# Taking two unread products out of the router stages of a hybrid decoder step

## The reference

```
u      = rmsnorm(h, norm_ffn[l]) * (1 + scale2) + shift2
g      = top-1 of 4 groups by softmax(u @ rg_w + rg_b)
e      = top-2 of the 4 experts of that group by softmax(u @ re_w + re_b)
weight = g_val * e_val / sum(e_val)
h1, h3 = u @ w1[expert], u @ w3[expert]          # 1024 -> 512
h      = h + gate2 * sum(weight * (silu(h1) * h3) @ w2[expert])
```

## Time and profile before

| what | value |
|---|---|
| device time, median of 3 runs | 963.4 us (963.22 to 965.36) |
| span of the profiled execution, first to last instruction | 961.9 us |
| TensorE busy in it | 908.2 us, 94% |
| TensorE weight loads | 498.1 us, 52% |
| VectorE busy | 321.1 us, 33% |
| ScalarE busy | 173.7 us, 18% |
| transfers | 316.22 MB, mean 329 GB/s |
| the product of `idle`, layer 0 | from 331.7 us, 4 instructions |
| the product of `idle`, layer 1 | from 711.6 us, 4 instructions |

### The profile page before, as it was taken

One profiled execution on the slowest core, in us unless ns is written; L12 is line 12 of the kernel. 1 busy time (PEld: TensorE's weight loads), 2 busy tenths in 40 slices (PEclk: granted clock), 3 DMA queues, 4 the chain that ended last, 5 costly groups with the idle time before them and its releaser, 6 DMA issues.

```text
span 961.9 us, 13150 instructions
## 1 busy us (share of the span) xinstructions
PE 908.2 (94%) x5368; PEld 498.1 (52%) x5368; DVE 321.1 (33%) x801; ACT 173.7 (18%) x385; POOL 40.0 (4%) x68
## 2 busy tenths in 40 slices
PE   6999999998889899999999989999989999999985
PEld 3665665453556654444444357776764444444533
DVE  3241135446524531112111077468462111211016
ACT  3200000022322221111111040173131110011103
POOL 0000000003300000000000110000000000000020
PEclk9999999998999999999999999999999999999998
DMA  9967987887977569999999987233848999999991
GB/s 374 420 282 263 352 311 265 323 312 264 402 288 306 219 241 421 424 420 421 422 421 423 377 333 279 88 134 135 350 176 335 417 422 421 423 423 420 422 358 66
DMA packets 47623, 316.22 MB, mean 329 GB/s; under 512 B 5602, under 2 KB 6002, under 8 KB 12354
## 3 DMA queue, kind: packets, MB, share of 16 engines
q1 hardware_dynamic: 39456, 288.90, 73.9%
q0 software_dynamic: 6096, 22.30, 6.4%
q10 hardware_dynamic: 2002, 4.08, 1.2%
HBM read 303.84 MB, written 11.42 MB: 328 GB/s over the span
## 4 chain that ended last, share of the span: by engine, by line
PE 78%; DMA 7%; SPq 6%; DVE 5%; issue 2%; ACT 1%; POOL 0%; POOLq 0%; DVEq 0%
PE banks L822 26%; PE banks L1446 14%; PE banks L1491 8%; PE banks L1405 7%; SPq L421 6%; PE banks L899 5%; DMA ring<-in_ew 3%; DMA scr<-in_ew 3%; PE banks L831 2%; PE banks L886 2%; PE banks L1462 1%; PE banks L907 1%; PE banks L939 1%; PE banks L963 1%; PE banks L1506 1%
## 5 line engine op out<-in xcount | busy, mean ns | idle before, releaser
L822 PE MATMUL banks<-uT,ring 128*128 128x320 f32 x448 | 124.5, 438 | 2.6 <-DVE uT L1700 2.6
L1446 PE MATMUL banks<-ring,scr 128*64 128x512 f32 x512 | 113.0, 593 | 1.7 <-issue 1.7
L822 PEld LDWEIGHTS banks<-uT,ring 128*128 128x128 f32 x448 | 85.6, 192 | 42.4 <-issue 7.0
L1405 PEld LDWEIGHTS banks<-scr 128*128 128x128 f32 (+1 forms) x768 | 75.3, 190 | 14.5 <-issue 12.4
L1446 PE MATMUL banks<-scr 128*64 128x512 f32 x352 | 78.1, 593 | 3.7 <-DMA scr<-in_ew 3.7
L1405 PE MATMUL banks<-scr 128*128 128x128 f32 (+1 forms) x768 | 81.4, 281 | 0.0
L1446 PEld LDWEIGHTS banks<-ring,scr 128*64 128x64 f32 x512 | 37.5, 137 | 74.6 <-issue 73.7
L619 ACT ACTIVATE scr<-banks,mods 128x128 f32<-128x128 f32 x128 | 36.5, 367 | 171.9 <-PE banks L1405 171.9
L1927 DVE TENSOR_TENSOR scr<-scr,banks 128x512 f32<-128x512 f32 x16 | 11.0, 687 | 156.7 <-ACT scr L605 156.7
L1491 PE MATMUL banks<-scr,uT 128*64 128x512 f32 x256 | 57.1, 596 | 0.0
L822 PE MATMUL banks<-ring,uT 128*128 128x512 f32 x128 | 57.1, 599 | 0.0
(11 more groups left out here) (381 smaller groups left out, 922.4 us busy)
## 6 DMA issues: line engine op xcount, KB each, us to landing
ring<-in_ew SPq DMA_DIRECT2D x112, 1024.0 KB, 21.2
ring<-in_w SPq DMA_DIRECT2D x80, 1024.0 KB, 8.7
scr<-in_ew SPq DMA_DIRECT2D x80, 1024.0 KB, 18.7
scr<-in_v POOLq DMA_DIRECT2D x16, 256.0 KB, 10.9
yd<-uT POOLq DMA_DIRECT2D x8, 512.0 KB, 8.5
scr<-in_kT POOLq DMA_DIRECT2D x13, 256.0 KB, 8.2
out_hgrn<-scr SPq DMA_DIRECT2D x1, 2304.0 KB, 10.6
scr<-in_s POOLq DMA_DIRECT2D x1, 2048.0 KB, 9.0
```

The source lines that it names most:

```text
L822: last = mm(out, a, b, start=(first and i == 0), stop=(final and i == len(pairs) - 1))
L1405: ins = mm(ps[h][:, PAIR * j:PAIR * j + PAIR], utok[r, t, P * d:P * d + P], pick[r, t, :, :].rearrange("p e n -> p (e n)"), start=first, s ...
L1446: ins = mm(ps[bank][SLOTS * x:SLOTS * x + SLOTS, :], xe[:, kk, SLOTS * x:SLOTS * x + SLOTS], wab[SLOT[n]][:, x, kk % 4, :], start=(kk == 0 ...
```

## The change

The function `idle` and its one call, at the end of `slots(l)`, are taken out. `slots` is called in both layers, so four products go, eight instructions in the profile.

```
-            def idle(n):
-
-                for _ in range(n):
-                    give(mm(ps[4][:, :], ident, const[:, 0:512], start=True, stop=True))
-
             def slots(l):
...
                 for n in range(4, 6):
                     tokens(l, n)
-                idle(2)
```

## The result

Without the two products the kernel is slower: 970.86 us median (966.78 to 976.08, 15 runs) against 965.22 us (962.92 to 972.23, 15 runs), ratio 1.0056 with a 95% interval of 1.0039 to 1.0073. That is 5.6 us lost, where 0.9 us was forecast as won.

The account below looks back on a forecast made before the run. It took TensorE's chain of waits through the two products into the gather as the bound, the weight stream following. 1.34 us won in layer 0 less 0.41 lost in layer 1 gave 963.4 - 0.9 = 962.5 us, range 960.5 to 965.0.

Parts of the forecast that it names:

- the change part by part: Router stages: products go, 5.50 us on the chain; gather then waits for VectorE and may run at low clock.
- low clock that comes to lie badly on a later stage: Stages after the gather: everything moves by a microsecond and low clock hits one; over 966.3 us, part of chance 0.07.
- The priced case on the slower side: Whole gather at 1.2 GHz in both layers: 9.72 us lost against 3.46 won, 969.7 us, chance 0.05.
- What bounds the kernel: TensorE's chain through products and gather; the weight stream moves with it, so a microsecond there is about one at the end.
- What is late next: Gather waits for VectorE's last token block, starting 1.99 and 1.47 us earlier: 3.46 us won at unchanged clock.
- The clock of the gather: Gather without the products runs partly at half clock: 1.34 us won in layer 0, 0.41 us lost in layer 1.
- The late rise: Clock stays low for 6.9 us, into the gather: net 0.41 us lost in a layer, taken for layer 1.
- the rival in which both rise late: Clock comes back late in both layers' gathers: 0.8 us lost, 964.2 us, chance 0.17.
- The rise in time: Clock rises in the gather where it rose before: net 1.34 us won in a layer, taken for layer 0.

Follow-up runs that it names:

- e2: Kernel before with the same two products moved ahead into TensorE's wait for the expert pick, in each layer: 963.80 us against 965.69, ratio 0.9969.
- e5: Kernel before with three products in the wait for the expert pick and one at the old place, in each layer: 961.44 us against 965.96, ratio 0.9951.
- e8: Kernel after with eight tiny instructions ahead of TensorE's first work: 965.92 us against 965.96 of before, ratio 1.0002.
- e9: Kernel after run once more, unchanged: 971.83 us against 965.99 of before, ratio 1.0054.
- e3: Kernel before with the two products kept in layer 0 and removed in layer 1 alone: 968.40 us against 965.69, ratio 1.0018.
- e1: Kernel after with eight tiny instructions in each layer, in TensorE's wait for the expert pick: 968.99 us against 965.69 of before, ratio 1.0038.
- e10: Kernel after with 64 tiny instructions ahead of TensorE's first work: 966.00 us against 965.99 of before, ratio 0.9997.
- e12: Kernel before with 228 tiny instructions ahead of TensorE's first work: 966.44 us against 965.99 without them, ratio 1.0003.

## Why the prediction was wrong

**The failed step** is the first of the change part by part: a few instructions go, "no wait, semaphore or DMA goes with them", and their price is the time that they took. (It also counted four in each layer; eight went, 13150 - 13134 = 16 in all.) Nearest came the "low clock that comes to lie badly on a later stage", part of a chance of 0.07: one did, at 352.9 to 356.3, but behind the stop and not by a shift of a microsecond. The priced case on the slower side, a gather wholly at 1.2 GHz, did not happen in any trace: the longest gather took 7.55 us (e2), and a whole one at half clock would take 9.7 (an estimate, twice 4.86).

**What bounds the kernel** was right. The products lay on the chain, and a microsecond there is one at the end: e5 wins 2.1 and 2.4 us in the two stages (to the end of the first hidden products) and 4.5 us in the median.

**What is late next** was right as to the wait: the gather waits for VectorE's last token block, with an idle time of 0.94 us, and starts 0.14 us after it ends (0.06 was taken). Its price holds where the clock falls late: in layer 0 of after the gather starts 2.1 us earlier than in before, counted from the first small product (1.99 forecast). In layer 1 it starts 0.14 us later (1.47 us earlier forecast), since the sum took the fall of the clock as fixed at its place in before.

**The clock of the gather** was right in its two prices and wrong in the choice. The late rise was priced at 0.41 us lost in a layer, with a low stretch of 6.9 us; e8, e9 and layer 0 of after show 0.3 to 0.4 us lost to the end of the gather, with 6.8 us. That is the rival in which both rise late. The rise in time, 1.34 us won, which the forecast took for layer 0, is in no trace without the products. Beyond both lies a low stretch of 10.2 us, after an early fall, which stands 1.7 to 2.0 us behind before (after and e3 in layer 1, e1 in both), though most of that goes with the fall. By time, the clock's share is what remains when the code is well placed: nothing in e8 and e10 (ratios 1.0002 and 0.9997), 3.3 us by the medians in e1 (1.0038). Whether e1's tiny products in the wait or chance made its early falls was not tried, so the share lies between 0 and 3.3 us, and nearer to 0 by the two kernels whose router stage is that of after.

**The sum.** 4.8 us for the code by the trace, and 0.3 to 0.4 us in each layer for the missing products after a late fall, make some 5.5, against 5.6 measured. Without the move of the code, by e8 and e10, the change would have been within 0.3% of before, where 0.84 of the chance lay, and the forecast of 0.9 us won would have been off by about 1 us; the code makes the rest.

**The rule on activity.** The Trainium skill (TensorE: Matmul & The Clock Gate, What's actually happening) has activity release the throttle, and the prediction weighed that as the case of both rising late. The traces without the products agree with it: after a late fall 6.8 us low where the products had 3.4, after an early one 10.2 where they had 6.8 (e10, 6.8, aside). In e5, with dense work in the wait, the clock did not fall in either layer.

## What to carry to other kernels

An edit that adds or removes instructions ahead of a branch moves the code behind it; before its own price is believed, look in the trace at the engine's first instructions after the branch, and for a gap of "issue" there that another padding takes away. When an edit moves a time by half a per cent for no visible reason, run it once more with a few dozen idle instructions at the program's start.

Work that is there only to keep the clock up belongs into the waits that the engine has anyway, ahead of the small products, not between the last input and the work that waits for it (e5; with two products there in place of three, e2, the clock fell in layer 0 all the same).

Before two traces are compared for what an edit does to the clock, see whether the clock fell at the same place in both: here that place alone was worth 1.2 to 1.6 us, more than the products.

## What the runs showed of the hardware

TensorE's branch ahead of the experts' code took 3.3 to 3.8 us in the sequencer (a row of one line's instructions, min/median/max ns); in the same trace the branches of ScalarE and VectorE took 0.04 to 0.07 us. A load of instructions begins 1.0 us after the branch does (346.89 against 345.89):

```profile
L1588 PEldq COMPARE_BRANCH  x2: 3329/3587/3845, 345.9 to 732.3; - x2
```

It goes unseen because the first half's 3.58 us of products are in the queue; the 0.5 to 1.4 us of stop in the table are what sticks out. The load of the block behind the entry begins about 0.7 us after the branch is through in after (349.96 against 345.89 + 3.33 = 349.22), and its first product starts 2.6 us later. In e12 the next block's first product also comes 2.2 us after its load begins (349.10 against 346.88), and ten products of work did not bridge the time. By these two traces, as an estimate, a branch whose target has less than some 3 us of work left in its block stops twice.

The times of one kernel spread by about 1% (before 962.9 to 974.8 in 35 runs; the three runs on which the prediction's 0.3% rested span 2.1 us). Part of it arises ahead of the router stage, where the clock falls at different places: the profiled execution of after was low there for 20.4 us and that of before for 13.7, which at half speed makes some 3.4 of the 5.1 us between them. What sets these places was not tried.
